# Two mixers with other group orders: first rotations in the sample's chain, state products between the inversion's levels

## The chip, the cores and the metric

The kernel runs on one core of one Trainium2 chip. The metric is the device time of one execution in microseconds, as the median of several runs.

## The reference, cut to what matters

One inference step of a two-layer trunk for 256 prompt tokens and 32 tokens of a running stream, width 1024, in float32. Each layer is a mixer and a mixture of experts with 32 experts, each followed by a residual sum.

```python
def run_trunk(x, pos, ...):
    for layer in range(DEPTH):                       # DEPTH = 2
        h = rmsnorm(x, norm_mix[layer])
        if layer % 2 == 0:
            out, c1, n1, m1, s1 = ab_mixer(h, pos, ...)   # mLSTM heads (A) and retention heads (B)
        else:
            out, s1, cv1 = gdn_mixer(h, gconv[j], ...)    # gated delta rule (C)
        x = x + out
        h = rmsnorm(x, norm_ffn[layer])
        x = x + hier_moe(h, ...)                     # two experts for each token
    y = rmsnorm(x, norm_final)

# in ab_mixer, the retention half: q and k are rotated by position first
    qb = rotary(to_heads(qb, H_B), pos)
    kb = rotary(to_heads(kb, H_B), pos) * DK_B ** -0.5
# rotary: concatenate([x1 * cos - x2 * sin, x1 * sin + x2 * cos])

# in gdn_scan, for a block of tokens with state s
    a = where(strict, bc[..., None] * einsum('bhid,bhjd->bhij', kc, kc) * gam, 0)
    u = triangular_solve(a + eye, vc * bc[..., None])
    w = triangular_solve(a + eye, kc * (bc * eg)[..., None])
    v_new = u - w @ s
    o = (qc * eg) @ s + (einsum('bhid,bhjd->bhij', qc, kc) * gam) @ v_new
    s = exp(g_last) * s + (kc * exp(g_last - G)).T @ v_new
```

The outputs are the trunk's values for all tokens and the new states of both mixers.

## The kernel before

All matrices are float32. The tokens form three tiles: 0 and 1 of 128 prompt tokens, 2 of the 32 sample tokens. The five queues (PE, ACT, DVE, POOL, SP) are written out by hand and meet through semaphores only: `wait` and `mark` or `signal` of an event `E[...]`. On ACT, DVE and POOL the helper `do` makes every instruction wait for the one before it.

PSUM's eight banks are handed out by lanes of two banks. `L0` (banks 0 and 1) is emptied by DVE, `L1` (2 and 3) by ACT, `background` (4 and 5) by ACT, `side` (6 and 7) by DVE. PE opens a bank with `open`, which waits until the filling two before it has been taken, and hands it over with `close`; the reader calls `take`.

The order in time is: mixer of layer 0 (`layer_ab`), its experts, mixer of layer 1 (`layer_c`), its experts, final norm. SP loads the weights in matrices of 2 MB into the slots of `W` and into scratch space. The experts' first matrices go where mixers have finished: `scratch_free` (the last flip of y: L1's count), `piece_done` (a projection's weights are used up), `states_out` (the states have been stored).

**First mixer, `layer_ab`.** The input projection has eight pieces of 512 columns; pieces 2 to 7 are projected token by token. A piece for one tile is eight steps of `project_gates` (k = 0 to 7). The table `BESIDE[t][i]` says which pieces PE projects at four points of the first pass of tile t: behind the row broadcast, behind `last_row`, inside `half` ahead of the wait for the scores, and ahead of `finish_half`. ACT takes a finished piece at the same points with `take_tokens` (an entry that ends before the last step is skipped). The first pass (f = 0) runs over tiles 0, 1, 2 for the mLSTM heads. The second (f = 1) runs over the tiles for the retention heads: DVE rotates q and k into `ab_rot` with 12 operations, with `GAM[1]` as scratch; PE flips them; DVE and ACT take `ab_q` and `ab_k`; `half` does the rest. PE projects piece 7 for tile 0 while DVE rotates tile 0.

**Second mixer, `layer_c`.** For a prompt tile the matrix I + A of each of 8 heads is inverted in blocks of 32: `block_scores`, then four levels (`block_level_y`, DVE masks it into `blkY`, `block_level_t`, DVE subtracts it from `blkT` and transposes), then `pairs_y`, `pairs_t`, `halves_y`, `halves_t`, which join blocks to 64 and 128. DVE marks each step with `yi_ready` and `tu_ready`, and ACT copies the blocks after `u_ready`. For tile 1 the output projection of tile 0 (`output_part(0, k)`, one k step of both halves of 512 columns) is spread over levels and joints. Behind the inversion stand two calls of `half` with `delta=True`, each with the whole chain: scores, keys times state, the flip of the scores, queries times state, new values, outputs, new state. Then come the flips of x, two `output_half` for tile 1 (k 0 to 3 and 4 to 7, into banks 6 and 7) and the router. POOL computes the inverse roots (`norm_tile`, `hrs`) and stores the states.

The new functions `state_products`, `second_tile`, `second_outputs`, `gate_gain` and `normed` stand in the diff below; `first_scores`, `first_scores_T`, `first_values` and `first_outputs` are the ones that tile 0 of the second mixer uses already.

## Time and profile before

| | us |
|---|---|
| median of 3 runs (1462.14 to 1463.89) | 1463.34 |
| profiled execution | 1466.4 |
| its span in the trace | 1464.6 |
| first use of the experts' buffers behind mixer 1 and 2 (SP issue) | 235.75, 978.27 |

| engine | busy us | share of the span |
|---|---|---|
| PE (matmul) | 1153.2 | 79% |
| DVE | 471.8 | 32% |
| ACT | 250.5 | 17% |
| POOL | 65.4 | 4% |

The span is the profiled execution from its first to its last instruction; times within it count from its start. Busy shares are averages over four stages of which each has limits of its own. The mean granted clock of TensorE was 0.909 of the full 2.4 GHz.

### The profile page before, as it was taken

To read this page: it belongs to the slowest core of one execution; us is meant where nothing else is said; L and a number is where in the kernel's file an instruction comes from. 1 tells how busy PE (TensorE), PEld (TensorE's weight loads), DVE (VectorE), ACT (ScalarE), POOL (GpSimd) and SP (SyncE) were. 2 spreads that over 40 slices of the span, in tenths; PEclk is the share of its full clock that TensorE was granted. 3 is DMA by queue.
4 is the path that set the end of the run, shared out by engine and by line. 5 is a ranking of instruction groups with operands and counts; after the bars stand their busy time and mean duration, and the time that the engine had idled before them with its cause. 6 is when DMAs were issued, how large, how long until landed. Compare 5 with 4: busy or idle time off the path is not lost.

```text
span 1464.6 us, 27531 instructions
## 1 busy us (share of the span) xinstructions
PE 1153.2 (79%) x11710; PEld 717.3 (49%) x11710; DVE 471.8 (32%) x1211; ACT 250.5 (17%) x633; POOL 65.4 (4%) x100
## 2 busy tenths in 40 slices
PE   8999889878585776775899989888867768767675
PEld 6645546444252443442478666556534434434342
DVE  1023445432232221322343746345222213222133
ACT  2123214110010100100232414131100101010011
POOL 2001102100000000000200101001000000000001
PEclk9999899998998887889899999999998879898888
DMA  9843235999999999999833303139999999999994
GB/s 274 184 92 112 77 122 224 420 411 428 427 429 429 429 428 430 426 429 430 258 120 115 117 4 130 60 118 380 424 428 427 428 428 429 428 430 428 428 428 190
DMA packets 54146, 453.87 MB, mean 310 GB/s; under 512 B 5680, under 2 KB 6480, under 8 KB 29760
## 3 DMA queue, kind: packets, MB, share of 16 engines
q1 hardware_dynamic: 52176, 448.35, 75.8%
q0 software_dynamic: 1904, 4.58, 1.2%
q8 instruction: 49, 0.80, 0.2%
q14 instruction: 17, 0.14, 0.0%
HBM read 449.55 MB, written 3.35 MB: 309 GB/s over the span
## 4 chain that ended last, share of the span: by engine, by line
PE 51%; DMA 38%; DVE 6%; issue 2%; ACT 1%; SPq 1%; POOL 1%; DVEq 0%; ACTq 0%; POOLq 0%
PE bank L341 49%; DMA W<-in_moe_w_up 37%; PE bank L344 1%; DMA W<-in_ab_w_in 1%; SPq L2484 1%; DVE zT L2332 1%; DVE HN L1593 0%; DVE HN L1573 0%; ACT zT L1538 0%; DVE gain L1573 0%; DVE HT L1573 0%; DVE zT L2337 0%; DVE X L1573 0%; DVE TM L1573 0%; DVE zT L1573 0%
## 5 line engine op out<-in xcount | busy, mean ns | idle before, releaser
L341 PE MATMUL bank<-W,zT 128*32 128x256 f32 (+1 forms) x6272 | 509.0, 454 | 171.1 <-DMA W<-in_moe_w_up 144.5
L341 PEld LDWEIGHTS bank<-W,zT 128*32 128x32 f32 (+1 forms) x6272 | 251.0, 127 | 386.6 <-issue 267.5
L2332 DVE TENSOR_TENSOR zT<-zT,bank 64x256 f32<-64x256 f32 x64 | 27.0, 422 | 408.1 <-ACT zT L1538 408.0
L341 PE MATMUL bank<-W,HT 128*32 128x128 f32 (+1 forms) x768 | 135.2, 398 | 3.3 <-ACT TM L1273 2.3
L341 PE MATMUL bank<-HT,W 128*128 128x288 f32 x512 | 126.9, 408 | 1.5 <-DMA W<-in_ab_w_in 1.5
L341 PEld LDWEIGHTS bank<-HT,W 128*128 128x128 f32 x512 | 96.6, 190 | 28.1 <-DMA W<-in_ab_w_in 2.0
L2342 DVE COPY zT<-bank 32x256 f32<-32x256 f32 x128 | 53.3, 416 | 156.8 <-PE bank L341 154.8
L341 PEld LDWEIGHTS bank<-zT,HN 128*128 128x128 f32 (+1 forms) x832 | 98.6, 195 | 9.7 <-issue 8.3
L341 PE MATMUL bank<-zT,HN 128*128 128x128 f32 (+1 forms) x832 | 101.5, 282 | 1.0 <-DVE HN L1573 0.7
L341 PE MATMUL bank<-const,zT 64*128 64x64 f32 (+3 forms) x340 | 47.6, 289 | 68.6 <-DVE zT L2332 68.2
L1544 ACT COPY zT<-bank 32x256 f32<-32x256 f32 x128 | 46.6, 364 | 264.2 <-PE bank L341 262.6
L341 PEld LDWEIGHTS bank<-W,HT 128*32 128x32 f32 (+1 forms) x768 | 62.4, 143 | 59.7 <-issue 54.7
L1538 ACT ACTIVATE zT<-bank 64x256 f32<-64x256 f32 x64 | 24.1, 377 | 393.1 <-PE bank L341 393.1
L341 PEld LDWEIGHTS bank<-const,zT 64*128 64x128 f32 (+2 forms) x340 | 37.2, 172 | 101.8 <-DVE zT L2332 78.2
L341 PE MATMUL bank<-zT,HT 128*32 128x256 f32 (+1 forms) x256 | 70.0, 509 | 16.5 <-DVE zT L2342 16.5
L341 PEld LDWEIGHTS bank<-zT,HT 128*32 128x32 f32 (+1 forms) x256 | 26.6, 152 | 56.7 <-issue 56.7
L1529 ACT ACTIVATE zT<-bank,gcol 128x128 f32<-128x128 f32 x64 | 18.3, 368 | 160.3 <-PE bank L341 160.3
L2373 DVE TENSOR_TENSOR X<-X,bank 128x512 f32<-128x512 f32 x64 | 40.5, 684 | 1.5 <-PE bank L341 1.0
L2563 POOL TENSOR_SCALAR sm<-sm 128x1 f32<-128x1 f32 (+3 forms) x21 | 5.4, 258 | 693.4 <-ACT zT L1205 468.5
L2337 DVE COPY zT<-bank 128x128 f32<-128x128 f32 x64 | 18.7, 292 | 50.5 <-PE bank L341 50.5
L341 PE MATMUL bank<-W 32*32 32x32 f32 (+3 forms) x1328 | 24.5, 199 | 9.3 <-DVEq L1588 7.0
L1265 ACT ACTIVATE zT<-bank 128x256 f32<-128x256 f32 x32 | 12.3, 384 | 111.7 <-PE bank L341 111.6
(285 smaller groups left out, 881.9 us busy)
## 6 DMA issues: line engine op xcount, KB each, us to landing
W<-in_moe_w_gate SPq DMA_DIRECT2D x62, 2048.0 KB, 18.0
W<-in_moe_w_up SPq DMA_DIRECT2D x62, 2048.0 KB, 22.5
W<-in_moe_w_down SPq DMA_DIRECT2D x62, 2048.0 KB, 22.4
W<-in_ab_w_in SPq DMA_DIRECT2D x8, 2048.0 KB, 16.5
W<-in_c_w_in SPq DMA_DIRECT2D x8, 2048.0 KB, 14.0
W<-in_ab_w_out SPq DMA_DIRECT2D x2, 2048.0 KB, 7.8
TM<-in_moe_w_gate SPq DMA_DIRECT2D x2, 2048.0 KB, 19.4
zT<-in_moe_w_up SPq DMA_DIRECT2D x2, 2048.0 KB, 15.3
```

Of the source, the lines that this page charges most:

```text
L341: return nc.tensor.matmul(out, lhsT, rhs, start=start, stop=stop)
L344: return nc.tensor.transpose(out, src, ident[:n, :n])
L1265: do(nc.scalar.activation(zT[:, c, PAD:PAD + 2 * P], bank[:, 0:2 * P], func, scale=scale))
L1529: nc.scalar.activation(xg[:, k, :], banks[1][:, (k - 4) * P:(k - 3) * P], ACT.Copy, scale=gcol[:, 4 + l, k:k + 1]).then_inc(m["xg_act"] if ...
L1538: nc.scalar.activation(sg[u % 2], banks[2 + u % 2][0:64, 0:2 * P], ACT.Silu).then_inc(m["silu"], 1)
L1544: ins = nc.scalar.copy(ys[BLK * u:BLK * u + BLK, 256 * c:256 * c + 256], banks[5 + u % 2][BLK * c:BLK * c + BLK, 0:256])
L2332: v.tensor_tensor(hid[u % 2], sg[u % 2], banks[2 + u % 2][64:128, 0:2 * P], ALU.mult).then_inc(m["hidden"], 1)
L2337: v.tensor_copy(hidT[u % 2], banks[4][:, 0:P]).then_inc(m["hiddenT"], 1)
L2342: ins = v.tensor_copy(ys[BLK * u:BLK * u + BLK, 256 * c:256 * c + 256], banks[5 + u % 2][BLK * c:BLK * c + BLK, 0:256])
L2373: v.tensor_tensor(x, x, banks[(5, 6, 7, 4)[i]][:, :], ALU.add).then_inc(m["added"], 1)
L2484: sp.dma_start(slots[k], flat).then_inc(moe[l]["w_in"][k], 16)
L2563: do(nc.gpsimd.tensor_scalar(src, src, scale, EPS, ALU.mult, ALU.add))
```

## The change

It has two parts.

First mixer: in the first pass of tile 2 the second half of piece 6 for tile 1 (steps 4 to 7) is cut into two pairs of steps, one behind `last_row`, one inside `half`. Piece 7 for tile 0 is projected ahead of the tile's `finish_half`, and ACT takes it at the start of the second pass, after it has marked `z_ready`. DVE rotates tile 0 right behind the diagonal of tile 2, with scratch of its own (`early_half`), and at the start of the second pass only signals.

Second mixer, tile 1: the products of the keys with the state (level 0), the scores (level 1), the queries with the state and the flips of the scores (level 2) stand between the levels, one group ahead of each block group; DVE handles each with one operation of `second_tile`, and scales the keys in level 3. The two `half` calls go; `first_values` and `first_outputs` follow the inversion. The eight `output_part(0, k)` stand behind the levels, one by one between the joints and the groups. The output of tile 1 goes to banks 4 and 5. `finish_half(1, 1)` moves ahead of the output's first half, and with it `scratch_free`; `flip_x(0)` moves between the two halves of the output. ACT squares only x of tile 2 early, x of tile 0 after y; POOL's `norm_tile(0)` moves behind the state.

```diff
           [[(4, 1, _LOW)], [(4, 1, _HIGH)], [], [(5, 2, _ALL), (5, 1, _ALL)]],
-          [[(6, 2, _ALL), (6, 1, _LOW)], [], [], [(6, 1, _HIGH)]]]
+          [[(6, 2, _ALL), (6, 1, _LOW)], [(6, 1, (4, 5))], [(6, 1, (6, 7))], [(7, 0, _ALL)]]]
...
         ab_rot = [heads4(ws[:, 5120 + 512 * i:5632 + 512 * i]) for i in range(2)]
+        early_half = heads4(ws[:, 2048:2560])
...
         b_end, c_ein, c_eout = small(16), small(64), small(64)
+        read_scale = ss_log[:, 0:8]
...
     for k in ks:
-        last = mm(banks[6 + p][:, :], zT[:, k, COL[t]:COL[t] + P], w[:, k, :], k == 0, k == KT - 1)
+        last = mm(banks[4 + p][:, :], zT[:, k, COL[t]:COL[t] + P], w[:, k, :], k == 0, k == KT - 1)
...
-def first_scores(f):
+def state_products(f, base):
...
     for h in range(4):
-        q, k = [zT[:, base + 4 * f + h, COL[0]:COL[0] + P] for base in (0, 8)]
+        last = mm(bank[:, h * P:h * P + P], zT[:, base + 4 * f + h, COL[1]:COL[1] + P],
+                  state1[:, 4 * f + h, :])
+    L0.close(last)
...
+def first_scores(f, t=0):
...
+    bank = L0.open(pe)
+    for h in range(4):
+        q, k = [zT[:, base + 4 * f + h, COL[t]:COL[t] + P] for base in (0, 8)]
...
                 output_part(t - 1, k)
-        else:
-            project_tokens([(7, 0, _ALL)])
...
     block_scores(1)
-    for lv in range(3):
-        output_part(0, 2 * lv)
-        block_level_y(1)
-        output_part(0, 2 * lv + 1)
-        block_level_t(1)
-    block_level_y(1)
-    output_part(0, 6)
-    block_level_t(1)
+    E["state_ready"].wait(pe)
+    for lv in range(4):
+        for f in range(2):
+            if lv == 0:
+                state_products(f, 8)
+            elif lv == 1:
+                first_scores(f, 1)
+            elif lv == 2:
+                state_products(f, 0)
+                first_scores_T(f)
+            (block_level_t if f else block_level_y)(1)
+    output_part(0, 0)
...
     E["u_ready"].wait(pe)
-    output_part(0, 7)
+    output_part(0, 1)
     pairs_t()
+    output_part(0, 2)
     halves_y()
+    output_part(0, 3)
     halves_t()
+    output_part(0, 4)
...
         E["tu_ready"].wait(pe)
-    E["state_ready"].wait(pe)
-    c = COL[1]
+    first_values()
+    output_part(0, 5)
     for f in range(2):
-        half(1, f, lambda h: zT[:, 4 * f + h, c:c + P], lambda h: zT[:, 8 + 4 * f + h, c:c + P],
-             16 + 4 * f, delta=True)
+        first_outputs(f)
+    output_part(0, 6)
+    output_part(0, 7)
...
     flip_x(2)
-    flip_x(0)
+    finish_half(1, 1)
+    scratch_free.append((L1.full.sem, L1.full.made))
     E["yT_act"].wait(pe)
-    E["out_taken"].wait(pe)
-    side.emptied(pe)
...
         output_half(1, p, range(4))
-    finish_half(1, 1)
-    scratch_free.append((L1.full.sem, L1.full.made))
+    flip_x(0)
...
         y_squares(n, 0, GAM[0])
-        take_tokens(BESIDE[t][3])
+        if t < 2:
+            take_tokens(BESIDE[t][3])
...
         if not t:
-            take_tokens([(7, 0, _ALL)])
+            take_tokens(BESIDE[2][3])
...
         bank = L1.take(act)
-        if t:
-            do(nc.scalar.copy(TM[:n, 20:24, :], heads4(bank[:n, :])), L1.taken)
-        else:
-            for h in range(4):
-                do(nc.scalar.activation(TM[:, 20 + h, :], bank[:, h * P:h * P + P], ACT.Copy,
-                                        scale=beta[:, 4 + h:5 + h]), L1.taken if h == 3 else None)
+        for h in range(4):
+            do(nc.scalar.activation(TM[:, 20 + h, :], bank[:, h * P:h * P + P], ACT.Copy,
+                                    scale=beta[:, 8 * t + 4 + h:8 * t + 5 + h]), L1.taken if h == 3 else None)
...
                     scores_T(n, first_ST[0])
+        else:
+            for f in range(2):
+                scores_T(n, first_ST[f])
...
         else:
-            for x in (2, 0):
-                x_ready.wait(act)
-                squares(x, ws[:, 0:1024])
-        if t == 0:
-            for f in range(2):
-                new_values(n, f)
+            x_ready.wait(act)
+            squares(2, gain[:, :])
         for f in range(2):
-            if t:
-                scores_T(n)
-                new_values(n, f)
-            y_squares(n, f, GAM[f] if t else first_ST[f], float(P) ** -0.5)
-            if not t and not f:
+            new_values(n, f)
+        for f in range(2):
+            y_squares(n, f, first_ST[f], float(P) ** -0.5)
+            if not f and not t:
...
         y_T(t, 0)
+        y_T(t, 1)
         if t:
+            x_ready.wait(act)
+            squares(0)
             take_x(0)
-        y_T(t, 1)
...
+def rotate(t, s):
...
+    n = N_TOK[t]
+    for j in range(2):
+        cos = bc_mid(rotc[:n, t, j, :], 4)
+        sin = bc_mid(rots[:n, t, j, :], 4)
+        x1, x2 = tok[t][:n, 8 + 4 * j:12 + 4 * j, 0:64], tok[t][:n, 8 + 4 * j:12 + 4 * j, 64:128]
+        o = ab_rot[j]
+        tt(o[:n, :, 0:64], x1, cos, ALU.mult)
+        tt(s[:n, :, 0:64], x2, sin, ALU.mult)
+        tt(o[:n, :, 0:64], o[:n, :, 0:64], s[:n, :, 0:64], ALU.subtract)
+        tt(o[:n, :, 64:128], x1, sin, ALU.mult)
+        tt(s[:n, :, 0:64], x2, cos, ALU.mult)
+        tt(o[:n, :, 64:128], o[:n, :, 64:128], s[:n, :, 0:64], ALU.add)
...
         diag(a3[:n, t, :], n)
+        if t == 2:
+            rotate(0, early_half)
...
         n, g = N_TOK[t], t // 2
-        for j in range(2):
-            cos = bc_mid(rotc[:n, t, j, :], 4)
-            sin = bc_mid(rots[:n, t, j, :], 4)
-            x1, x2 = tok[t][:n, 8 + 4 * j:12 + 4 * j, 0:64], tok[t][:n, 8 + 4 * j:12 + 4 * j, 64:128]
-            o, s = ab_rot[j], GAM[1]
-            tt(o[:n, :, 0:64], x1, cos, ALU.mult)
-            tt(s[:n, :, 0:64], x2, sin, ALU.mult)
-            tt(o[:n, :, 0:64], o[:n, :, 0:64], s[:n, :, 0:64], ALU.subtract)
-            tt(o[:n, :, 64:128], x1, sin, ALU.mult)
-            tt(s[:n, :, 0:64], x2, cos, ALU.mult)
-            tt(o[:n, :, 64:128], o[:n, :, 64:128], s[:n, :, 0:64], ALU.add)
+        if t:
+            rotate(t, GAM[1])
...
         bank = L0.take(dve)
+        tt(TM[:, 16:20, :], heads4(bank[:, :]), bc_last(beta3[:, t, 0:4], P), ALU.mult, L0.taken)
         if t:
-            cp(TM[:n, 16:20, :], heads4(bank[:n, :]), L0.taken)
+            tt(read_scale, negbeta3[:, 1, :], c_out[:, 1, 24:32], ALU.mult)
+            signal(E["state_ready"])
         else:
-            tt(TM[:, 16:20, :], heads4(bank[:, :]), bc_last(beta3[:, 0, 0:4], P), ALU.mult, L0.taken)
...
         for lv in range(4):
+            if t:
+                second_tile(lv, 0)
...
                  lambda: first_scores(1))[lv]()
+            else:
+                second_tile(lv, 1)
...
         signal(E["yi_ready"])
-        if not t:
+        if t:
+            gate_gain(0)
+        else:
...
         if t:
-            add_output(0)
+            gate_gain(1)
...
         if t:
-            signal(E["state_ready"])
             for f in range(2):
-                o = lambda w: c_out[:, t, w + 4 * f:w + 4 * f + 4]
-                half(t, f, GAM[f][:n, :, :n], o(0), o(8), o(16), 8 + 4 * f, 16 + 4 * f, delta=o(24),
-                     between=first_norm if f else None)
+                second_outputs(f)
...
         if t:
-            E["gates_ready"].wait(dve)
-            head_norm(t, (1,), (0, 4), 0, (2, 0))
+            for f in range(2):
+                normed(f)
+                if not f:
+                    take_x(2)
+            add_output(0)
+            take_x(0)
...
         x = X[:, 1, 512 * p:512 * p + 512]
-        tt(x, x, banks[6 + p][:, :], ALU.add)
+        tt(x, x, banks[4 + p][:, :], ALU.add)
...
-def first_norm():
+def second_tile(lv, f):
...
+    col = lambda w: c_out[:, 1, w + 4 * f:w + 4 * f + 4]
+    if lv == 3:
+        tt(first_kw[f], TM[:, 8 + 4 * f:12 + 4 * f, :], bc_last(col(8), P), ALU.mult, E["kw_ready"])
+        return
+    bank = L0.take(dve)
+    if lv == 0:
+        v_ = TM[:, 16 + 4 * f:20 + 4 * f, :]
+        by_head(v_, heads4(bank[:, :]), read_scale[:, 4 * f:4 * f + 4], v_, ALU.mult, ALU.add, L0.taken)
+        if f:
+            signal(E["r_ready"])
+    elif lv == 1:
+        tt(first_S[f], heads4(bank[:, :]), GAM[f], ALU.mult, L0.taken)
+        signal(E["s_ready"])
+    else:
+        tt(Yout[:, 4 * f:4 * f + 4, :], heads4(bank[:, :]), bc_last(col(0), P), ALU.mult, L0.taken)
...
+def second_outputs(f):
...
+    y = Yout[:, 4 * f:4 * f + 4, :]
+    bank = L0.take(dve)
+    tt(y, heads4(bank[:, :]), y, ALU.add, L0.taken)
+    signal(E["y_done"])
+    st = state1[:, 4 * f:4 * f + 4, :]
+    bank = L0.take(dve)
+    by_head(st, st, c_out[:, 1, 16 + 4 * f:20 + 4 * f], heads4(bank[:, :]), ALU.mult, ALU.add, L0.taken)
...
+def gate_gain(f):
     E["gates_ready"].wait(dve)
-    head_norm(1, (0,), (0, 4), 0)
+    g = TM[:, 4 * f:4 * f + 4, :]
+    tt(g, g, bc_mid(hgain[:, 0, :], 4), ALU.mult)
...
+def normed(f):
...
+    y = Yout[:, 4 * f:4 * f + 4, :]
+    E["hrs_ready"].wait(dve)
+    by_head(y, y, hrs[:, 4 * f:4 * f + 4], TM[:, 4 * f:4 * f + 4, :], ALU.mult, ALU.mult)
+    signal(E["y_ready"])
...
                 norm_tile(2)
-                norm_tile(0)
...
                 E["state_done"].wait(pool)
+            else:
+                norm_tile(0)
```

## Rows read from the trace of the kernel before

**Rows 1.** The page's bars, mean busy share of the DMA engines in 40 slices.
```profile
DMA  9843235999999999999833303139999999999994
```

**Rows 2.** Timeline of SP, DMA issues: start, us, queue, line, operation, destination and source, count.
```profile
235.75 0.33 SPq L2484 DMA_DIRECT2D W<-in_moe_w_gate  x1
...
978.27 0.33 SPq L2484 DMA_DIRECT2D W<-in_moe_w_down  x1
...
1011.82 0.33 SPq L2484 DMA_DIRECT2D W<-in_moe_w_gate  x1
```

**Rows 3.** Busy time in a stretch at the second mixer's end, columns as named.
```profile
core 0: us, PE busy (x) PEld busy (x) DVE busy (x) ACT busy (x) POOL busy (x), PEclk, DMA share, GB/s
...
1008.00:1011.80 3.80, 3.79 (x65) 1.91 (x64) 3.28 (x16) 2.42 (x5) 0.00 (x0) 1.00 0.54 211
```

**Rows 4.** Timeline of PE, first mixer: start, us, form, count, idle before and releaser.
```profile
148.96 0.44 PE L341 MATMUL bank<-zT 128*32 128x32 f32 x8 [1.35 <-DVEq L1588]
151.33 0.39 PE L344 MATMUL bank<-const,HN 32*32 32x32 f32 x4 [1.93 <-DVEq L1588]
...
159.81 5.65 PE L341 MATMUL bank<-W,HT 128*128 128x512 f32 x8
...
166.63 7.13 PE L341 MATMUL bank<-W,HT 128*128 128x512 f32 x16 [0.80 <-ACTq L1353]
...
175.46 1.13 PE L341 MATMUL bank<-W 128*128 128x128 f32 x8 [0.83 <-DVEq L1588]
```

**Rows 5.** Busy time and granted clock in three stretches, columns as in rows 3.
```profile
150.00:155.00 5.00, 3.11 (x23) 2.60 (x24) 2.18 (x6) 1.00 (x4) 0.00 (x0) 0.51 0.00 0
...
222.00:229.00 7.00, 6.12 (x49) 4.26 (x48) 3.27 (x8) 1.42 (x9) 0.00 (x0) 1.00 0.01 2
919.20:939.70 20.50, 18.06 (x566) 9.78 (x567) 5.15 (x12) 0.00 (x0) 0.00 (x0) 1.00 0.20 81
```

**Rows 6.** Timeline of DVE, first mixer.
```profile
141.90 0.28 DVE L1573 TENSOR_TENSOR W<-bank,const 32x128 f32<-32x128 f32 x1 [5.52 <-PE bank L341]
...
166.61 0.88 DVE L1573 TENSOR_TENSOR W<-TM,const 128x256 f32<-128x256 f32 x2 [4.48 <-ACTq L1353]
```

**Rows 7.** Timeline of ACT, first mixer.
```profile
166.63 1.28 ACT L1326 ACT_TABLE_LOAD   x1 [0.17 <-ACT zT L1283]
...
174.73 0.59 ACT L1359 COPY W<-bank 128x512 f32<-128x512 f32 x1 [0.34 <-PE bank L344]
```

**Rows 8.** Timeline of PE, second mixer.
```profile
855.96 1.08 PE L341 MATMUL bank<-W 32*32 32x32 f32 x64
...
917.41 1.99 PE L341 MATMUL bank<-W,zT 128*128 128x512 f32 x4
...
922.90 0.72 PE L341 MATMUL bank<-W 32*32 32x32 f32 x60 [0.74 <-issue]
...
926.75 0.18 PE L341 MATMUL bank<-W 32*32 32x32 f32 x1 [0.54 <-issue]
...
948.86 2.05 PE L341 MATMUL bank<-zT 128*128 128x128 f32 x8 [1.81 <-DVEq L1588]
...
958.34 1.16 PE L341 MATMUL bank<-zT 128*128 128x128 f32 x8
...
970.77 7.03 PE L341 MATMUL bank<-W,zT 128*128 128x512 f32 x16
```

**Rows 9.** Timeline of DVE, second mixer.
```profile
918.55 0.45 DVE L1985 STREAM_TRANSPOSE W<-W 128x256 f32<-128x256 f32 x1
...
939.27 0.45 DVE L1996 STREAM_TRANSPOSE W<-W 128x256 f32<-128x256 f32 x1
...
952.54 1.13 DVE L1593 SCALAR_TENSOR_TENSOR HN<-bank,sm,TM 128x128 f32<-128x128 f32 x4 [0.91 <-PE bank L341]
...
986.21 0.69 DVE L1573 TENSOR_TENSOR X<-X,bank 128x512 f32<-128x512 f32 x1 [2.82 <-PE bank L341]
```

**Rows 10.** DMA issues: bytes of one, median us from issue to landing.
```profile
out_gdn<-HN POOLq DMA_DIRECT2D x1, 512.0 KB, 4.3
...
small_w<-in_c_w_in POOLq DMA_DIRECT2D x1, 64.0 KB, 17.6
```

## Prediction, made before the changed kernel was run

> **What bounds the kernel now.** I read the bars of the page first. The 16 DMA engines are full in two long blocks (the experts) and mostly idle in two stretches (the mixers) [rows 1]; each slice is 36.6 us. Next the sync engine's queue: a block of weights starts when a mixer releases its last buffers, at 235.75 and 978.27 us, and in the second layer it goes on when the first expert has used its gate matrix, at 1011.82 us [rows 2]. So the time is four stages in a row, and what a mixer gains moves everything behind it, unless the weights come late already. At the end of the first mixer the DMA engines fill up from the release on, and the release moves with the mixer [rows 1, 2]; at the end of the second they are busy 0.54 of the time just before 1011.8 us, so TensorE and the router set that point [rows 3]. Last came the timelines of PE, DVE and ACT round the two places that the change touches. The profiled execution took 1466.4 us for a span of 1464.6 us, 3.1 us over the median of 1463.34 us; I take the sum off the median. A change within 0.2% (2.9 us) can hardly be told from none.
>
> **First mixer, sample tile.** PE waits 1.35 us and 1.93 us while the other engines handle 32 tokens [rows 4]. Its clock is halved there: 0.51 granted from 150 to 155 us [rows 5], and the four steps of piece 6 that follow take 5.65 us where eight steps at full clock take 7.13 [rows 4]. Behind them PE runs piece 7 for tile 0 (from 166.63 us) while DVE rotates from 166.61 us, and then flips the result [rows 4, 6].
>
> The change puts two steps of piece 6 ahead of each of the two waits, and piece 7 where the four steps were. The 12 rotation operations (0.44 us each, 5.5 us with gaps) go behind the sample's diagonal, where DVE idles 5.52 us [rows 6], since PE still has projections in front of the product that DVE awaits. So they cost nothing; without that cover they would cost their 5.5 us. PE's order at full clock, 0.89 us a step: last row done at 147.6 us; two steps, 149.4; scores, 149.8; two steps, 151.6 (0.3 us later than the flip now, the price of the second insertion); then flip, state products, sums and values. Piece 7 can start near 157.2 instead of 159.81 us, because these products now run at half clock. It takes 7.2 us; the flip of y ends at 164.8, ACT has copied and signals at 165.4.
>
> PE then flips the rotated halves at once. The first product of the second pass starts at 175.46 us now; the new one waits for ACT, which loads a table (1.28 us) and takes piece 7 (as long as a copy, 0.59) before its own copy [rows 4, 7]: with the hand-overs 2.75 us, so 168.15. That is 7.3 us gained if the clock stays full. I don't think it does: from 151.6 to 157.2 only thin products are left, as in the stretch that lost it, though a like stretch at 222 to 229 us kept 1.00 [rows 5]. One return to half that ends inside piece 7, over some four of its steps and the products ahead, costs 2.2 us. I take **5.1 us**; bounds 1.8 (clock down from 150 us on, as now) and 7.3.
>
> **Second mixer, tile 1: the levels.** From DVE's first transpose (918.55) to the end of the fifth (939.7) the four levels take 20.7 us from 919.0, with six output parts of tile 0 of 1.98 us between them [rows 8, 9]. Now they hold six groups of eight full products (1.16 us at full clock) and two groups of flips instead, with one operation of DVE for each group: two sums by head (1.13 us each), four multiplications (0.69 each), and two key scalings (0.69) with no group [rows 8, 9]. The limit is the lane of two banks: a group opens only when the fill two before it has been taken. With 0.45 us for a mask, a subtraction or a transpose [rows 9] and the hand-overs of 0.1, level 0 takes 4.6 us (DVE: 1.13 + 0.45 + a wait of 0.75 for the second group + 1.13 + 0.45 + 0.45), level 1 the same with 0.69 for 1.13, 3.9 with its first wait; level 2 has a flip of 0.45 ahead of each block group, 4.6; level 3 (0.69, 0.45, 0.69, 0.45, 0.45) 3.1. Sum 16.2 us, from 919.1 (0.1 for the read scale and ACT's four copies with beta) to 935.3.
>
> **From there to the last projection.** Now 939.7 to 970.77 us [rows 8, 9]: the solve's groups, then two chained halves in which PE waits six times, 1.81 us at the first [rows 8]. After, PE from 934.2: eight parts 15.6, the four solve groups 3.5, values 2.0, outputs 4 x 1.05 and 0.15 of waiting, first flip 0.6, sample flips 0.75, a wait of 1.75 (DVE takes the sample's x before it scales the second half, 1.14), flip 0.6: 29.2, so 963.4 us. The solve's own waits lie beside the parts. Then 7.1 for eight steps, 0.95 for the flip of x tile 0, moved between, and 7.1: the last bank at 978.5, where DVE now starts its last addition at 986.21 [rows 9]. That is 7.7 us. In the old levels PE's sequencer also stalled twice, 0.74 and 0.54 us [rows 8]; I expect as much in the shorter chain and subtract 1.3: **6.4 us**.
>
> The output of tile 1 in banks 4 and 5 drops a wait for the take of tile 0. I cost it at nothing: eight steps of 7.1 us would lie beside that take. On the queues: SP's two matrices behind the second flip move from 978.27 to 963.5, then it waits for the output pieces as before. POOL now scales tile 0 behind the state and only then stores it (about 967 us); behind the store stand ACT's rows of tile 0 and, on SP, the scattered matrix. The same store took 4.3 us, the slowest small transfer beside weights 17.6 [rows 10]. The first is nearest: landed at 972, before ACT comes to it (974). With 17.6 it would be 985 and tile 1's squares some 5 us late, which I keep for the upper end.
>
> Between 960 and 963.4 us PE has little to do, so another spell at half clock there is about as likely as not, for some 1.7 us in the steps behind it; I subtract 0.7. **Sum: 5.1 + 6.4 - 0.7 = 10.8 us; 1463.3 - 10.8 = 1452.5 us.**
>
> The old levels held 1.00 from 919.2 to 939.7 us, with the output parts in them [rows 5]. The Trainium skill speaks against thinner ones: TensorE: Matmul & The Clock Gate, section "A second HAM failure mode: psum-queue depth-cycling", tells of a kernel that cycles through PSUM banks, pauses between groups and swings between the clock's two levels. By that rule the time would be that of rival 2; by the row, the sum above.
>
> **Rivals.** (1) The clock holds in the sample's tile, because the inserted steps keep PE at work: 2.2 us more gain and perhaps the 0.7: about 1449.5 us. For it 222 to 229 us, against it 150 to 155 [rows 5]. (2) The thinned levels fall to 1.2 GHz. Each of six groups costs 0.9 more (2.05 against 1.16 us), the eight block groups 0.35 each (1.08 against 0.72 for nearly as many), the first part 1.9 [rows 8]: 5.4 + 2.8 + 1.9 = 10.1, so 1462.6 us. (3) The hand-overs eat what the levels lose, and these stay at 20.7 us: 4.5 us less gain, 1457 us. For it: every group now waits for DVE; against it: DVE works 5.15 us of 20.5 there now [rows 5]. (4) Slower: half clock through all of 919 to 963 us. To the 10.1 it adds 7 more parts x 1.9 and about 6 for values and outputs, 29 us in all: some 1482. It decides against the change once it covers about 22 us of work that PE alone bounds; the spell in the first mixer lasts under 15 us, so it is unlikely. (5) The gain is hidden because weights come late: 1463. [rows 3] speaks against it.
>
> **Chances.** Forecast 0.55, (1) 0.15, (2) 0.12, (3) 0.10, (4) 0.04, (5) 0.04. The range may leave out 0.2: it holds the forecast, (1) and (3), with the 7.3 at one end and the late store at the other: 1446 to 1459 us. Faster by over 0.2% (below 1460.4): forecast, (1), (3) and over half of (2) by its spread, 0.87. Same: 0.08. Slower: 0.05.
>
> **What would show it.** DVE's rotation of tile 0 from 136.4 us, over before the sample's product comes; piece 7 near 157 us; the first product of the second pass at 168 to 171, behind ACT's table load. In the second mixer the transposes' span 16 us, the clock near 1.00 there; parts between the solve groups; a wait of 1.7 us ahead of the second flip of y; the last output 6 to 8 us sooner, counted from the start of the levels. The expert stages keep their length. I am wrong if the clock falls inside the levels, if DVE waits over 1 us for each group, if ACT's rows wait for the store, or if the weights' stage takes back what the mixers gave.

## Result and the profile after

| | before | changed |
|---|---|---|
| median, us | 1467.74 (20 runs, 1459.81 to 1477.88) | 1460.93 (20 runs, 1454.45 to 1469.99) |
| profiled execution, us | 1466.4 | 1463.67 |
| its span, us | 1464.6 | 1461.8 |

The ratio is 0.995, with a 95% interval of 0.9933 to 0.9968: of 1467.7 us that is 7.3 us less (4.7 to 9.8; the two medians are 6.8 us apart). The prediction said 10.8 us less, and 1452.5 us with a range of 1446 to 1459. The time lies 1.9 us above that range, and the reason is in two parts. The kernel before takes 1467.7 us over 20 runs and not the 1463.3 us that the sum started from, which is 4.4 us; and the gain is 3.5 us smaller than forecast.

The DMA bar of the changed kernel's page shows the same two full blocks and the same two thin stretches as [rows 1]:

```profile
DMA  9752233999999999999923302248999999999995
```

The release of the first layer's last buffers comes at 242.03 us, 6.3 us later than in [rows 2], though the execution is shorter:

```profile
242.03 0.33 SPq L2548 DMA_DIRECT2D W<-in_moe_w_gate  x1
```

The first mixer is where the profile speaks against the forecast. PE's timeline there (start, us, form, count, idle before and its releaser), to be read beside [rows 4]:

```profile
149.01 0.38 PE L343 MATMUL bank<-sm,const 32*128 32x8 f32 x2
149.32 1.98 PE L343 MATMUL bank<-W,HT 128*128 128x512 f32 x4
151.24 0.44 PE L343 MATMUL bank<-zT 128*32 128x32 f32 x8
...
155.73 2.11 PE L343 MATMUL bank<-zT,HN 32*32 32x128 f32 x16 [0.71 <-DVE HN L1585]
157.79 1.86 PE L343 MATMUL bank<-const,HN 32*128 32x1 f32 x8
159.58 9.61 PE L343 MATMUL bank<-W,HT 128*128 128x512 f32 x16
...
170.17 1.06 PE L346 MATMUL bank<-const,W 128*128 128x128 f32 x8 [0.62 <-ACTq L1368]
172.72 1.13 PE L343 MATMUL bank<-W 128*128 128x128 f32 x8 [1.49 <-issue]
...
176.44 3.78 PE L343 MATMUL bank<-TM,HN 128*128 128x128 f32 x16 [0.72 <-ACTq L1317]
180.15 9.73 PE L343 MATMUL bank<-W,HT 128*32 128x128 f32 x80
192.76 1.09 PE L346 MATMUL bank<-const,W 128*128 128x128 f32 x4 [2.88 <-issue]
193.64 9.56 PE L343 MATMUL bank<-W,zT 128*128 128x512 f32 x16
```

The two steps of piece 6 fill each wait as foreseen. Piece 7 starts at 159.58 and takes 9.61 us instead of 7.13, and the first product of the second pass comes 23.7 us behind the sample's last row (149.01, the sample's own gate row, which I use as the local origin: the mixer is 1.8 us late here, and was so before the first edited place). Before, that distance was 28.2 us (from 147.23). So 4.5 us are gained up to here. From that product to the release it is 69.3 us against 60.3 before, so 9.0 are lost again, in groups such as the last row's: 16 matmuls of 512 columns take 9.56 us that take 7.03 in [rows 8]. The granted clock says why. Busy time by stretch, columns as in [rows 3]:

```profile
150.00:155.00 5.00, 5.00 (x36) 2.61 (x34) 1.59 (x7) 2.56 (x8) 0.00 (x0) 1.00 0.23 43
157.80:164.60 6.80, 6.80 (x15) 3.96 (x15) 3.90 (x12) 1.28 (x8) 3.17 (x5) 0.50 0.49 185
174.80:181.60 6.80, 6.08 (x48) 5.36 (x52) 2.01 (x3) 1.87 (x9) 0.72 (x2) 0.50 0.00 0
191.90:198.70 6.80, 5.94 (x10) 2.93 (x11) 5.80 (x15) 0.59 (x1) 0.00 (x0) 0.50 0.96 402
...
229.40:236.20 6.80, 6.80 (x20) 4.12 (x19) 4.24 (x11) 1.28 (x8) 2.03 (x3) 0.50 0.02 7
```

It holds 1.00 from 150 to 155 us, where [rows 5] have 0.51, and then stands at 0.50, the 1.2 GHz level, in four later stretches of 6.8 us, the last of them behind the rows shown above. I call such a stretch a spell. The rotation isn't to blame: DVE does it in the gap of [rows 6], where the sample's product keeps it idle anyway, and ACT's table load of [rows 7] is where the sum has it:

```profile
138.20 0.88 DVE L1585 TENSOR_TENSOR W<-TM,const 128x256 f32<-128x256 f32 x2
```

```profile
170.07 1.28 ACT L1340 ACT_TABLE_LOAD   x1 [0.17 <-ACT zT L1297]
```

In the second mixer the forecast held better. DVE's timeline from the first transpose, beside [rows 9]:

```profile
923.53 0.45 DVE L2006 STREAM_TRANSPOSE W<-W 128x256 f32<-128x256 f32 x1
924.01 1.13 DVE L1605 SCALAR_TENSOR_TENSOR TM<-bank,sm,TM 128x128 f32<-128x128 f32 x4
...
928.00 1.13 DVE L1605 SCALAR_TENSOR_TENSOR TM<-bank,sm,TM 128x128 f32<-128x128 f32 x4 [2.41 <-PE bank L343]
...
931.38 0.69 DVE L1585 TENSOR_TENSOR HN<-bank,W 128x512 f32<-128x512 f32 x1 [1.09 <-PE bank L343]
...
942.67 0.45 DVE L2021 STREAM_TRANSPOSE W<-W 128x256 f32<-128x256 f32 x1
...
986.04 0.69 DVE L1585 TENSOR_TENSOR X<-X,bank 128x512 f32<-128x512 f32 x1 [2.82 <-PE bank L343]
```

And PE's, beside [rows 8]:

```profile
927.36 0.60 PE L343 MATMUL bank<-HN,zT 128*128 128x128 f32 x4 [1.46 <-issue]
...
929.18 2.08 PE L343 MATMUL bank<-zT 128*128 128x128 f32 x8 [0.54 <-DVE TM L1605]
...
968.96 0.66 PE L346 MATMUL bank<-const,W 128*128 128x128 f32 x4 [1.81 <-DVEq L1600]
969.45 8.73 PE L343 MATMUL bank<-W,zT 128*128 128x512 f32 x16
```

From the first to the last transpose the levels take 19.1 us (20.7 before, 16.2 forecast). From the last transpose to the first group of tile 1's output it is 26.8 us (31.5 before). First transpose to that group: 45.9 us against 52.2, so 6.3 us gained. The group itself meets a spell at half clock (8.73 against 7.03 us) and gives 1.7 back. From the first transpose to the last addition of DVE it is 62.5 against 67.7 us, each with 6.8 us of half clock in it (twice the length times what the granted clock, last but two and rounded in the rows, lacks to 1). First the kernel before, then the changed one:

```profile
918.55:986.21 67.66, 56.40 (x814) 35.90 (x813) 27.81 (x64) 15.50 (x35) 4.87 (x9) 0.95 0.20 76
```

```profile
923.53:986.04 62.51, 55.71 (x808) 35.33 (x808) 26.46 (x63) 15.21 (x35) 4.88 (x9) 0.95 0.31 117
```

At the second mixer's end the DMA engines are idle where [rows 3] have them at 0.54, so no weight is late there, and the store of [rows 10] lands later:

```profile
1006.00:1010.00 4.00, 3.99 (x67) 2.00 (x65) 3.48 (x16) 2.43 (x5) 0.00 (x0) 1.00 0.01 2
```

```profile
out_gdn<-HN POOLq DMA_DIRECT2D x1, 512.0 KB, 10.8
```

### The profile page after: what moved, and what is told of

The parts are those of the page before. It is cut to its first block, busy times and chain, and to the rows that moved or that the text cites. A ratio compares the mean times of both kernels' runs of the same rounds, so it can differ in the third digit from the quotient of the medians.

```text
span 1461.8 us, 27531 instructions
## 1 busy us (share of the span) xinstructions
PE 1149.9 (79%) x11710; PEld 714.1 (49%) x11710; DVE 471.1 (32%) x1210; ACT 252.1 (17%) x636; POOL 65.1 (4%) x100
## 4 chain that ended last, share of the span: by engine, by line
PE 55%; DMA 35%; DVE 6%; issue 2%; ACT 1%; SPq 1%; POOL 0%; DVEq 0%; ACTq 0%; POOLq 0%
PE bank L343 53%; DMA W<-in_moe_w_up 33%; PE bank L346 2%; DMA W<-in_ab_w_in 1%; DVE zT L2396 1%; SPq L2548 1%; ACT zT L1550 1%; DVE HT L1585 0%; DVE zT L2401 0%; DVE gain L1585 0%; DVE W L1585 0%; DVE zT L2406 0%; DVE HN L1585 0%; DVE zT L1585 0%; DVE W L1605 0%
## 5 line engine op out<-in xcount | busy, mean ns | idle before, releaser
L343 PEld LDWEIGHTS bank<-W,HT 128*32 128x32 f32 (+1 forms) x768 | 62.4, 143 | 58.9 <-issue 54.9
L343 PE MATMUL bank<-zT,HT 128*32 128x256 f32 (+1 forms) x256 | 73.1, 534 | 16.4 <-DVE zT L2406 16.4
L343 PE MATMUL bank<-W 32*32 32x32 f32 (+3 forms) x1352 | 27.6, 202 | 8.2 <-DVEq L1600 5.2
L343 PEld LDWEIGHTS bank<-W 32*32 32x32 f32 (+3 forms) x1352 | 23.9, 114 | 17.6 <-DVEq L1600 9.4
```

Source lines behind the costliest of these rows:

```text
L343: return nc.tensor.matmul(out, lhsT, rhs, start=start, stop=stop)
```

## The experiments

Theory 1 is that the re-ordering did what the prediction said, and that the rest is the granted clock of TensorE: PE still waits in new and old places of the chain, and how much half clock a first mixer gets differs between executions. The rival of each run is in its expectation. In the diffs "+" is what the experiment adds to the kernel named. All were timed against the kernel before, except the last two.

**First and second part alone.** The first takes the `BESIDE` table, `rotate` and `early_half` alone; the second undoes these in the changed kernel:

```
-          [[(6, 2, _ALL), (6, 1, _LOW)], [(6, 1, (4, 5))], [(6, 1, (6, 7))], [(7, 0, _ALL)]]]
+          [[(6, 2, _ALL), (6, 1, _LOW)], [], [], [(6, 1, _HIGH)]]]
...
-                    if t == 2:
-                        rotate(0, early_half)
```

> Only the first mixer's part: rotations, pieces 6 and 7 and ACT's takes as in the changed kernel; the second mixer as before. Theory 1, clock: the chain to the first product of the second pass is 4 to 5 us shorter, but PE now idles in new places there, falls to half clock behind them, and gives it back; time -1 to +2 us against before, and the profile shows spells at half clock between 170 and 200 us. Theory 2, order: the part gains its 4 to 5 us also in the median, the profiled execution was an unlucky one; then this kernel is at -4 to -6 us.

> Only the second mixer's part. Theory 1: it holds nearly all of the gain, -6 to -8 us. Theory 2: -2 to -4 us, what is left when the first part has its 5. By itself the profile should show some 65 us from the block scores of tile 1 to the last addition for tile 1, where before shows 69.5.

First alone: 1465.58 us, ratio 0.9978 (0.9955 to 1.0001), 3.2 us less, with an interval from 6.6 to nothing. That lies between the two forecasts (+2 to -1 and -4 to -6 us) and settles neither; the spells came where theory 1 put them, at 178 and 195 us. Second alone: 1464.49 us, 0.9956 (0.9927 to 0.9985), 6.5 us less. The second part measures its 6.4 us. The profiles agree: from the first transpose to the last addition the four with the old second mixer take 67.7, 69.5, 68.6 and 68.8 us, with 6.8 to 10.2 us at half clock, and the five with the new one that no later edit touches 62.5 to 62.6 us, with 3.4 to 6.8. The first part alone measures less than its 5.1, though 5.1 is within the interval. In the second kernel's profile the old first mixer took 240.8 us from the first weights to the release, where the profile that the prediction read has 231.6. These rows of PE are of the same code as [rows 4] and behind them:

```profile
166.85 7.13 PE L343 MATMUL bank<-W,HT 128*128 128x512 f32 x16 [0.81 <-ACTq L1369]
...
183.11 9.73 PE L343 MATMUL bank<-W,HT 128*32 128x128 f32 x80
```

The spells are therefore not the new order's alone.

**Unread products in PE's waits.** `keep` issues products of a constant with itself into a bank that nobody reads; they change no value. The first run puts them in the first mixer's waits, the second in the second's, with seven more ahead of the second router's choice, the third in all of these:

```
+            def keep(n, bank=7):
+                for _ in range(n):
+                    mm(banks[bank][:, 0:P], tri_incl, tri_incl)
...
+                if t == 0 and f == 1:
+                    keep(3)
                 E["s_ready"].wait(pe)
...
+                if (t, f) in ((2, 0), (0, 1)):
+                    keep(2)
...
+                    if not t:
+                        keep(2)
                     E["rot_ready"].wait(pe)
...
+                    if not t:
+                        keep(5)
                     E["qkT_dve"].wait(pe)
...
                        project_tokens([(7, 2, _ALL), (7, 1, _ALL)])
+                        keep(10)
...
+                        keep({(0, 1): 3, (1, 0): 2, (3, 0): 2, (3, 1): 4}.get((lv, f), 0), 5)
...
                 flip_x(2)
+                keep(6, 5)
                 finish_half(1, 1)
...
-                idle_products(14)
+                idle_products(21 if l else 14)
                 E["choice_ready"].wait(pe)
```

> The changed kernel with dense products that nobody reads in PE's waits of the first mixer: 2 ahead of the values of the sample tile, then in tile 0 of the second pass 2, 5, 3 and 2, and 10 ahead of its flip of y. Theory 1: the clock stays full between 165 and 200 us (at most one spell left, round the sample's thin products), and the kernel is 4 to 6 us faster than the changed one, so -11 to -13 against before. Theory 2: no change to the changed kernel within 1 us, since the clock is not what the first part lacks.

> The changed kernel with such products in the second mixer: 11 in the waits of the levels, 6 ahead of the second flip of y, 7 more ahead of the router's choice. Theory 1: no spell at half clock in the levels nor in front of the output halves; 2 to 3 us less than the changed kernel. Against it: the levels wait for two banks and DVE, then they keep their 19 us and the kernel its time, apart from 1.7 us behind the second flip of y.

> The changed kernel with the unread products of both earlier fill runs (first mixer's waits, second mixer's waits, the router's). Clock theory: what each gave against the changed kernel adds up, -0.3% each, so about 0.989 of before (-15 to -17 us), with one spell at most in the first mixer's second pass and one in the second mixer behind the rotations. Rival: both earlier gains were the luck of few runs; then 0.992 to 0.995.

| kernel | us | ratio to before | less than before, us |
|---|---|---|---|
| changed | 1460.93 | 0.995 (0.9933 to 0.9968) | 7.3 |
| filled, first mixer | 1456.97 | 0.9919 (0.9888 to 0.995) | 11.9 |
| filled, second mixer | 1456.55 | 0.992 (0.9888 to 0.9952) | 11.7 |
| filled, both | 1452.38 | 0.9895 (0.986 to 0.9931) | 15.4 |

More instructions make the kernel faster. Against the changed kernel each filling is worth 4 to 5 us by the ratios, and both together 8.1. The interval of each alone overlaps that of the changed kernel; the one of both just clears it, and the version with both beats both kernels. In the first mixer the profile is as forecast, with one spell (160.6 to 167.4 us). In the second the gain is not located: from the first transpose to the last addition the two kernels take 61.9 and 60.7 us instead of 62.5, the first of them still has a spell of 3.4 us in its levels, which the forecast excluded, and the seven products ahead of the router were not timed apart. The levels of the kernel with both hold 1.00 and still take 19.0 us, with a wait of PE in them for which the profile names no releaser:

```profile
918.47 0.94 PE L343 MATMUL bank<-zT 128*128 128x128 f32 x6 [1.68 <-issue]
```

**The same filling in the kernel before.** If it is the clock, it must help there too. `keep(5)` and `keep(7)` go into the two waits of the sample's tile where the change has piece 6, with two products ahead of its values as above; tile 0 of the second pass has 3, 3, 2 and 10 in its waits:

```
+                    if t == 2:
+                        keep(5)
                     E["state_ready"].wait(pe)
...
+                keep({(2, 0): 7, (0, 1): 3}.get((t, f), 0))
                 E["s_ready"].wait(pe)
...
+                    if not t:
+                        keep(3)
                     E["qkT_dve"].wait(pe)
```

> The kernel before with unread products in the waits of its own first mixer: 5 and 7 in the two waits of the sample tile where the change puts piece 6, 2 ahead of its values, 3, 3 and 2 in tile 0 of the second pass, 10 ahead of its flip of y; the second mixer untouched. Clock theory: the old order gains from a full clock as the new one does, 4 to 6 us (0.996 to 0.997), as much as the changed first part gains in all or more. If it is the place of the real steps that counts and not the clock, no change within 1 us, or slower by the products' own 3 us.

1459.71 us, 0.9941 (0.9911 to 0.9971): 8.7 us less (4.3 to 13.1, where 4 to 6 were forecast), as much as the whole change, without any of its re-ordering. PE's timeline and the clock of the stretch of [rows 5]:

```profile
149.87 1.83 PE L341 MATMUL bank<-const 128*128 128x128 f32 x14
...
157.12 3.70 PE L341 MATMUL bank<-W,HT 128*128 128x512 f32 x8
...
161.99 7.13 PE L341 MATMUL bank<-W,HT 128*128 128x512 f32 x16 [0.64 <-ACTq L1366]
...
170.82 1.13 PE L341 MATMUL bank<-W 128*128 128x128 f32 x8 [0.16 <-issue]
...
185.01 2.39 PE L341 MATMUL bank<-const 128*128 128x128 f32 x20
```

```profile
150.00:155.00 5.00, 4.76 (x46) 4.16 (x46) 2.52 (x8) 1.50 (x5) 0.00 (x0) 1.00 0.00 0
```

Four steps take 3.70 us instead of the 5.65 of [rows 4], piece 7 comes 4.6 us sooner, and the first product of the second pass stands 23.1 us behind the last row (147.76): 5.2 us of the 28.2 go with the order unchanged, once the clock is full. The changed order needs 22.1 us in its second profile below, 1.5 of them lost to half clock in piece 7 (8.66 against 7.13 us). At full clock the re-ordering gives some 2.5 us up to that product, not 5.1 to 7.3.

**Three edits on the chain.** The table load of [rows 7] moved ahead of the rotated flips; in the second mixer the second half of y ahead of the sample's x; and in the last kernel both, with both fillings, and the state's store ahead of the scale of tile 0:

```
+                    else:
+                        do(nc.scalar.activation(blank_out, ones[:, 0:1], ACT.Silu))
                     y_T(t, 0)
...
                 finish_half(1, 0)
-                flip_x(2)
                 finish_half(1, 1)
+                flip_x(2)
...
-                            if not f:
-                                take_x(2)
+                        take_x(2)
...
+                            store(a["out_gdn"][0].rearrange("h k v -> k h v"), states[1])
                             norm_tile(0)
-                    store(a["out_gdn"][0].rearrange("h k v -> k h v"), states[1])
```

> The changed kernel; ACT loads the Silu table by a one-column operation before it waits for the sample's flip of y, not behind the mark. The wait of PE between the flips and the first product of the second pass shrinks from 2.55 us by about 0.7 to 1.3 us. If the table on ACT's chain is what ate the first part, the gain goes on to the end (0.7 to 1 us less than the changed kernel, 0.9945 of before); in the clock theory it also makes one wait shorter in front of the spell, so perhaps 2 us. Nothing of it can explain 5 us.

> The changed kernel with the sample's x behind the second scaling on DVE, and its flips behind the second flip of y on PE. The wait of 1.81 us ahead of that flip goes, and with it the spell at half clock in the output steps (1.7 us): 1.5 to 3.5 us faster than the changed kernel, 0.993 of before. If DVE's scale waits for POOL's roots instead, nothing changes.

> The changed kernel with the unread products of the two filled runs, and three more edits on the chain: ACT's table load ahead of the rotated flips, the normed second half of y ahead of the sample's x in the second mixer, and the state's store ahead of the scale of tile 0. Theory 1 (the clock set the loss, and the chain is what is left once it holds): the edits add to the filled kernel, each by 1 to 2 us, so 0.987 of the kernel before, with the first product of the second pass 1.2 us sooner behind its flips and two matrices of weights issued 1.1 us sooner in the second mixer. Rival (the gains seen for the table load and the order of y in their own runs were spread of the clock): 0.9895, as the kernel with both fillings, within 0.2%.

Alone they gave 1458.45 us, 0.9937 (0.9913 to 0.9961), and 1458.52 us, 0.9923 (0.9895 to 0.9951), against 0.995 for the changed kernel: both better by less than the intervals can part. Their rows moved as expected: with the table early the first product of the second pass stands 1.89 us behind the start of its flips and not 2.55, and with y first PE's wait of 1.81 us is gone and the way from the first transpose to the last addition takes 58.9 us and not 62.5, with 3.4 us of half clock in it and not 6.8. On top of both fillings the three gave 1453.21 us, 0.9903 (0.9869 to 0.9937), beside 0.9895: no gain seen. That is the rival's forecast, though the interval just reaches theory 1's 0.987. The rows say what became of each edit. In the first mixer the filled kernel runs unread products in the wait that the table load had lengthened, so the first product came 1.99 us behind its flips instead of 2.10, where 1.2 us were expected. In the second the two matrices were issued 25.7 us behind the last transpose instead of 27.0, as expected, but in this execution the levels before it had a spell and took 20.2 us instead of 19.0. The store's row moved too, and that leads to nothing. ACT's first rows of tile 0 now follow on its other rows with no wait for the store:

```profile
957.37 0.95 POOL L2639 DMA_DIRECT2D out_gdn<-HN  x1 [0.30 <-POOL sm L2730]
```

```profile
969.73 4.17 ACT L1270 ACTIVATE HN<-X,sm 32x1024 f32<-32x1024 f32 x2
```

In the changed kernel they had waited for it, with the store issued at 973.06 us:

```profile
984.30 2.05 ACT L1254 ACTIVATE HN<-X,sm 128x1024 f32<-128x1024 f32 x1 [2.38 <-POOLq L2723]
```

but ended at 986.35 us, just as DVE made its last addition (986.04), for which ACT's next work waits anyway.

**Fewer columns in the unread products.** The same count in the same places, with 4 columns read instead of 128:

```
-                    mm(banks[bank][:, 0:P], tri_incl, tri_incl)
+                    mm(banks[bank][:, 0:4], tri_incl, tri_incl[:, 0:4])
```

> The kernel with both fillings, but each unread product reads 4 columns instead of 128: the same count of instructions in the same places, with little work in them. Theory 1 (it is dense work in the waits that keeps the clock): the gain of the filling is gone, 0.995 of the kernel before, and second-pass groups of 9.6 to 10 us with spells of half clock at 150 to 200 us are back. Rival A (any instruction in the waits does it, or they act by shifting PE's order): 0.9895, as with 128 columns, and groups of 9.0 us. Rival B (the thin products only lengthen the queue): slower than the changed kernel, 0.997.

1457.13 us, 0.9915 (0.9886 to 0.9945). That lies between the forecasts: of the 8 us that both fillings give over the changed kernel, 5 stayed by the ratios and 4 of 8.6 by the medians. The interval holds rival A's 0.9895, ends just below theory 1's 0.995, and overlaps that of the changed kernel. The profile leans to theory 1: a spell is back over the products behind `rot_ready` (first fence), and the clock was at 0.50 for 10 us round the end of the levels (second fence; the last transpose is at 935.28 us). This execution took 1464.4 us against a median of 1457.1.

```profile
168.63 1.18 PE L343 MATMUL bank<-const 128*128 128x4 f32 x10
...
173.71 3.78 PE L343 MATMUL bank<-TM,HN 128*128 128x128 f32 x16
177.42 9.60 PE L343 MATMUL bank<-W,HT 128*32 128x128 f32 x80
186.86 2.29 PE L343 MATMUL bank<-const 128*128 128x4 f32 x20
```

```profile
933.00:943.20 10.20, 9.77 (x119) 4.43 (x117) 2.99 (x6) 3.56 (x8) 0.75 (x2) 0.50 0.01 2
```

The run doesn't part the theories as hoped, for a reason that the rows show: `keep(10)`, which is 20 matmuls in them, keeps PE busy for 2.29 us with 4 columns and for 2.39 us with 128 (the last row of the filled kernel before, above). The control took away the columns and not the busy time.

**Both kernels once more.**

> The kernel before, unchanged, in a second profiled execution. Theory 1 says that the profile of before that the prediction read was a favourable one in the first mixer: 231.6 us from the first block of weights to the release of the last, with one spell of 13.7 us of half clock before 240 us. Here it should be 234 to 241 us with three or more spells (240.8 us in the kernel with the second part alone, which has the same first mixer), and the first product of the second pass in the same place from the last row. Rival (the old order holds its clock better there, and the changed second mixer moved the spells of the first by chance of alignment alone): within 1 us of 231.6.

> The changed kernel, unchanged, in a second profiled execution. Theory 1: the first mixer's stage scatters between executions as its spells do, 230 to 238 us where the first profile had 237.9 (231.8 and 226.3 us in runs that differ from it only behind this place or by a table load). The levels of the second mixer hold 18.5 to 19.5 us again, since there it is hand-overs and not the clock that set them. Rival (the order fixes the spells): 237.9 within 1 us, with spells at 158, 175 and 192 us again.

The kernel before took 232.8 us to the release, 1.2 us from the profile that was read: theory 1's 234 to 241 missed, as did the rival's 1 us by a little, and its "favourable profile" stands on one execution out of three. The changed kernel took 228.1 us where its first profile has 237.9: the scatter that theory 1 said, 1.9 us beyond the lower end of its range, and the rival's 237.9 is out. The levels took 18.2 us, a little under its 18.5 to 19.5, with 2.0 us of half clock in them. PE's rows of this second profile:

```profile
154.88 2.11 PE L343 MATMUL bank<-zT,HN 32*32 32x128 f32 x16 [0.71 <-DVE HN L1585]
...
158.03 8.66 PE L343 MATMUL bank<-W,HT 128*128 128x512 f32 x16
...
170.24 1.13 PE L343 MATMUL bank<-W 128*128 128x128 f32 x8 [1.49 <-issue]
...
175.57 9.02 PE L343 MATMUL bank<-W,HT 128*32 128x128 f32 x80
```

The waits are the same to a hundredth (0.71, 1.49 us), and the clock is not. With fourteen profiles the first mixer can be laid out by its clock. The table has the length of the way from the sample's last row to the release and the time at half clock in it (the sum of its stretches). Here are the rows of four of them, in the order: before again, before filled, changed, changed again:

```profile
147.88:236.99 89.11, 75.51 (x364) 43.81 (x364) 42.52 (x106) 15.52 (x56) 9.24 (x13) 0.92 0.22 82
```

```profile
147.76:231.11 83.35, 77.38 (x428) 47.68 (x428) 42.54 (x106) 15.52 (x56) 9.24 (x13) 1.00 0.24 88
```

```profile
149.01:242.03 93.02, 82.06 (x364) 47.14 (x364) 37.41 (x94) 15.56 (x56) 8.83 (x13) 0.85 0.21 78
```

```profile
148.16:232.22 84.06, 73.11 (x364) 41.27 (x364) 37.43 (x94) 15.51 (x56) 9.24 (x13) 0.96 0.23 86
```

| order of the first mixer | us at half clock | last row to release, us |
|---|---|---|
| old, filled | 0 | 83.4 |
| old, before and again | 13.7, 13.7 | 88.5, 89.1 |
| old, second part alone | 30.7 | 96.7 |
| new, table load early; the same, filled | 3.4, 3.4 | 81.8, 82.2 |
| new, again; two filled | 6.8, 6.8, 6.8 | 84.1, 84.0, 84.0 |
| new, filled with 4 columns | 10.2 | 85.2 |
| new, second filled; y first | 13.7, 13.7 | 86.6, 86.6 |
| new, first part alone | 17.1 | 88.2 |
| new, changed | 27.3 | 93.0 |

Each microsecond at half clock costs 0.43 us in both orders ((96.7 - 83.4) / 30.7, and (93.0 - 84.1) / (27.3 - 6.8)), and at 13.7 us of it the new order is 2.2 us shorter than the mean of the old. That is the size of the first part, from two profiles against two: 2.2 us by order, and 0.43 us for each microsecond of half clock gained or lost, which scattered in both orders (13.7 to 30.7 us and 3.4 to 27.3 us in the kernels unfilled there).

The granted clock that each timed run reports for the whole program agrees for the fillings: 0.9014 on average in 68 runs of the kernel before, 0.9026 in the 20 of the changed one, 0.9047 to 0.9082 in the five kernels with products of 128 or 4 columns in the changed order, and 0.9063 for the filled kernel before.

## Why the prediction missed

- **The base.** The sum was taken off 1463.34 us, the median of three runs. Over 20 runs it is 1467.74, 4.4 us more, and the profiled execution (1466.4) was the nearer one: the sum off that would have been 1455.6 us. The three runs lay within 1.8 us of each other and said nothing of a spread that reaches over 18 us in twenty. This is over half of the miss of 8.4 us, and by itself it put the time outside the range: the same sum and the same range off 1467.7 us would be 1457 us and 1450 to 1463, which holds 1460.93.
- **First mixer, 5.1 us: the term that failed.** The rotation went where it was put (DVE from 138.20 to 143.7 us, ahead of the sample's product), piece 7's idle lead is gone, and the first product came 4.5 us sooner by the local origin; the forecast for it, 20.9 us behind the last row at full clock, was near what the rows give (22.1 us less 1.5). But the step compared a stretch that the profile shows at half clock with one supposed at full, and called the difference the order's. The filled kernel before has full clock and the old order, and it takes 23.1 us where the prediction read 28.2. "One return to half that ends inside piece 7" is where the sum stopped counting; the rows show three more spells behind it in the first profile (174.8, 191.9 and 229.4 us) and one in the second. By the laid-out profiles the order is worth 2.2 us; alone the part measured 3.2 (0 to 6.6). The lower bound of 1.8 was the nearer one.
- **Second mixer, 6.4 us: right,** 6.5 us alone (2.2 to 10.7), though put together otherwise. The levels took 19.1 us instead of 16.2, or 19.0 in the filled kernel, whose levels hold full clock throughout: hand-overs and PE's waits without a named releaser, not the clock. DVE waits 6.3 us there in all in the changed kernel, some 3 us more than the sum has, the longest time 2.41 us with such a wait of PE of 1.46 us in it. The stalls of 1.3 us that I subtracted as a lump were of that size. From the last transpose on it was shorter than forecast, 26.8 against 28.5 us, mostly because the eight parts took 14.6 us of PE and not 15.6. The kernel before was no clean base here either: it has 6.8 us at half clock from 945 to 952 us, over the last joint and the first chained half. The changed kernel has as much elsewhere, so the 5.2 us between the two first profiles are at equal clock; the 6.1 us between the means of all profiles hold some clock, since three of the old ones have 10.2 us of it. That the whole came to 6.4 is in part luck: 2.9 us lost in the levels stand against 1.7 gained behind them and the lump of 1.3.
- **The wait ahead of the second flip of y:** 1.75 us forecast, 1.81 us measured. **The spell behind it:** forecast as likely as not, 1.7 us; 8.73 against 7.03 us in the first profile.
- **Banks 4 and 5 at no cost:** the rows show no wait ahead of either output group but the flips' own. **POOL's store:** it landed after 10.8 us and not 4.3, and held ACT's rows until 984.30 us, which cost nothing since DVE's last addition came later still.
- **The rivals.** (2), thin levels falling to half clock, came true for one stretch (929.2 to 932.6 us, eight products in 2.08 us) and not for all. The Trainium skill tells of such swings with short pauses between groups (TensorE: Matmul & The Clock Gate, "A second HAM failure mode: psum-queue depth-cycling"). The trace agrees in part: in the first mixer, where the prediction did not apply it, groups with pauses of 0.6 to 2.9 us swing between 1.00 and 0.50, and the levels, where it did, held 1.00 but for 3.4 us. (3), hand-overs that eat the gain, is what the levels did by 3 of 4.5 us, with the later part giving 1.7 back. (4) and (5) did not come: the experts took 420.3 and 451.8 us against 423.3 and 452.7.

Of the prediction's signs of being wrong three came, at least in part, and none of them made the miss: the clock fell in the levels for 3.4 us, DVE waited over 1 us ahead of two of their groups (2.41 and 1.09 us), and ACT's rows waited for the store.

The Trainium skill, on the same page, section "HAM oscillation — how this bites in real kernels", tells of a kernel that loses the clock while it waits for DMA between bursts, and advises an order in which PE stays busy. The trace shows the loss in a chain whose waits are of 0.6 to 2.9 us, and filling those gave 4 to 5 us for each mixer of the changed kernel.

**What stays open.** Whether the new order brings more or less half clock on average than the old: six profiles of it unfilled there have 3.4 to 27.3 us (mean 13.7), three of the old 13.7 to 30.7. Whether unread products act by PE's busy time or by their columns: 4 columns kept about half of the gain, with an interval that overlaps both kernels'. Where the second filling's 4.4 us lie, of which the profiles show 0.6 to 1.8 in the stretch that it fills. And which wait starts a spell, since equal waits did in one execution and not in another.

## What to carry to other kernels

Where the granted clock of a stretch is below 1 in the profile, price a re-ordering at equal clock first, and give the clock a term of its own with the time at half clock that the stretch could have, not the time that one profile shows. Before re-ordering a chain full of waits, put unread products into the waits: it is a few lines, gave as much here (8.7 us, 4.3 to 13.1) as the whole change, and adds to it. And where single executions scatter over 18 us, three runs that agree make no base.

## What the runs showed that I had not expected

- Twenty matmuls of 32-bit numbers with 4 columns take 2.29 us and with 128 columns 2.39 us: between 4 and 128 columns the columns hardly set the time.
- The runs of the kernel before spread from 1459.8 to 1480.1 us, with the work of every queue in the same order. In the profiles of the first mixer the spread is that of the half clock.
- The same store of 512 KB landed after 4.3, 10.8 and 3.9 us in the kernel before, the changed kernel and the last one, where it was issued 8 us ahead, 3 us behind and 3 us ahead of the weights.
